# Block 2's state-space stage over 80 units with paired products, the second attention and the gated unit moved behind

## The chip, the cores and the metric

One NeuronCore of a Trainium2 chip runs the whole kernel. The metric is the device time of one execution in microseconds. TensorE multiplies, VectorE (DVE) and ScalarE (ACT) work on tiles in SBUF and PSUM, GpSimd (POOL) on tiles in SBUF, and the SP queue issues the loads of the weights.

## The reference, cut to what matters

Two transformer-like blocks in fp32, on 256 tokens of width 2048. The change is in the second one's mixers:

```python
def second_block(x, ...):
    h = rmsnorm(x, norm1_g)
    proj = h @ w_in                      # 2048 x 12288: uv, s5_in, q, k, v and three gates
    y_a = gmlp_mixer(uv, ...)            # u * (tril(W_s) rmsnorm(v) + b), chunks of 128 tokens
    y_b = s5_mixer(s5_in, ...)           # the state-space stage
    y_c = stick_breaking_attention(q, k, v)      # 8 heads of 128
    br = einsum('blnw,nwd->blnd', stack([y_a, y_b, y_c]), w_branch)
    x = x + sum(gates * br) @ w_out
    h2 = rmsnorm(x, norm2_g)
    x = x + square(relu(h2 @ w_mlp_in)) @ w_mlp_out

def s5_mixer(xin, ...):                  # 64 groups of 16 channels, each with 64 complex states
    bu_re, bu_im = einsum(u, bb_re), einsum(u, bb_im)        # products in, K = 16 per group
    s = associative_scan(s[t] = a * s[t-1] + bu[t])          # complex, over 256 tokens
    y = einsum(s_re, c_re) - einsum(s_im, c_im) + d * xin    # products out
    g = gelu(y)
    return g * sigmoid(g @ w_glu + b_glu)
```

## The kernel before

**Units.** All large products run as "units": a load of 128x1024 fp32 weights by the SP queue into `raw` (a ring of 4), a rounded high half `whi` on ScalarE, the rest `wlo` on VectorE (L946), and 12 matmuls of 128x512 on TensorE (high by high, high by low, low by high). Unit i's high half waits until unit i-4 is multiplied, so ScalarE and VectorE can be at most some three units ahead. There are 1048 units. Block 2's first phase holds 120: 96 for the projections s5, q, k, v, gv, u (two chunks of 8 units each), then 24 for three chunks of gates.

**The order.** Everything else is written by hand as generators that say `yield p`: on each engine, step p of a generator comes behind unit p of that engine (its high half on ScalarE, its low half on VectorE, its matmuls on TensorE), counted from the start of the phase. Within a step the generators run in a fixed order; on VectorE the evictions come first, then the state-space stage, the attention, the gated unit. A step that waits holds up everything behind it on its engine, the next half or unit too.

**The state-space stage** has 32 tiles of 128 states (real and imaginary). Tile j: TensorE puts B·u into bank `PU[j % 2]` (K = 32 rows at a tile position, `s5_in`, step S5Q + 2j, S5Q = 26); VectorE turns it by a table of angles (L1312, L1313 read PSUM and the table; L1315, L1316 combine) and scans over time (L1320, L1321, `ROT`), step S5Q + 2j + 2; GpSimd turns it back into `STATE` (L468 to L471); for each pair of tiles TensorE multiplies by C into `PT[1][:, 0:T]` (`s5_out`, step S5Q + 4m + 9, four column groups of 32); for every four tiles VectorE adds d·x (`skip`, L1328) and releases the bank (`s5_y`). The tables come by SP loads into a ring of 5 in tile G. The stage ends at step 90.

**The second attention** (`attn2`, head h at q0 = HQ2 + 6h, HQ2 = 57): scores into `PT[0]`, Abs, Exp, Ln on ScalarE, L1336 to L1338 on VectorE, the triangle products on TensorE at q0 + 3, Exp on ScalarE, the product with v into `PT[1][:, T:2T]` at q0 + 6, and the high and low half of the result (`y_lo`, L1055) at q0 + 8. `PT[1]` is one bank shared by `s5_out` and this product. So the product waits for the `skip` of all quads multiplied out by then, and `s5_out` for the `y_lo` of the last head.

**The gated unit** (`gmlp`, GQ = 104): squares and root for the norm, the scaling with the gain GMG, four mixing products, the multiplication by u, four transposes. **The gates' evictions** (L1019) read the biases, for n = 0 from `slot(W, 7, 2)`, which is the stage's scratch until its end, and write `GT[k]`, slots of G where the tables lie.

Of the kernel before, what the change touches and what calls it, by code (L numbers as in the profile page):

```python
# [21 lines left out]
P = 128  # L22
# [27 lines left out]
def build(nc, A, out):  # L50
    with ExitStack() as ctx:
# [163 lines left out]
        def yready(b, k):  # L215
# [22 lines left out]
        GMG = slot(W, 6)  # L238
# [20 lines left out]
            slot(W, 8)[:, 0:512], slot(G, 2)[:, 512:1024], slot(Z, 5)[:, 512:1024], slot(Z, 11)[:, 512:1024])]  # L259
# [3 lines left out]
        S5Q, HQ2, GQ = 26, 57, 104  # L263
# [18 lines left out]
        def bias_buf(n, k):  # L282
            if n == 0:
                return slot(W, 7, 2)[:, CH * k:CH * k + CH]
            return slot(W, 12)[:, CH * ((3 * n + k) % 2):CH * ((3 * n + k) % 2) + CH]
# [41 lines left out]
        def _(sp_):  # L327
# [6 lines left out]
            def tables():  # L334

                for j in range(S5_TILES):
                    yield S5Q + 2 * j + 1 if j >= NTAB else 6 + j
                    if j == 0:
                        sp_.wait_ge(S("tables_saved"), 32 * S5_TILES // TG)
                    if j >= NTAB:  # L340
                        sp_.wait_ge(S("s5_state_ready"), j - NTAB + 1)
                    sp_.dma_start(TAB[j % NTAB], A["tables"][j]).then_inc(S(f"table_in{j % NTAB}"), 16)
# [41 lines left out]
        def _(pool):  # L384
# [59 lines left out]
            def block2():  # L444

                pool.wait_ge(S("vA_ready"), 1)
                pool.wait_ge(used, mlp_base(1, NF - 1))
                bsrc = BSRC
                for r, name in enumerate(("s5_b_re_2", "s5_b_im_2")):
                    pool.dma_start(bsrc[:, r], A[name][0].rearrange("(j g) p h -> (g p) j h", g=2)).then_inc(S("small2_in"), 16)  # L450
                csrc = CSRC
                for r, name in enumerate(("s5_c_re_2", "s5_c_im_2")):
                    pool.dma_start(csrc[:, r], A[name][0].rearrange("(i g) h q -> (g h) i q", i=8)).then_inc(S("small2_in"), 16)
                gw = GWSRC
                pool.dma_start(gw, A["gm_w_s_2"][0].rearrange("g t s -> t g s")).then_inc(S("small2_in"), 16)
                pool.wait_ge(evict["dve"], down0[1] + NF * NCH)
                pool.dma_start(A["x1"].rearrange("(t p) n -> p t n", p=P), X).then_inc(S("x_saved"), 16)
                pool.wait_ge(S("small2_in"), 16 * 5)
                nc.gpsimd.affine_select(out=gw, in_=gw, compare_op=ALU.is_ge, fill=0.0, base=0,
                                        pattern=[[0, 8], [-1, P]], channel_multiplier=1).then_inc(S("gm_w_tril"), 1)  # L460
                for j in range(S5_TILES):

                    tab, r, state = TAB[j % NTAB], ROT[j % 2], STATE[j % NS]
                    c, s = (tab[:, i].unsqueeze(1).to_broadcast([P, 2, T]) for i in range(2))
                    pool.wait_ge(S("s5_r_ready"), j + 1)
                    if j >= NS:
                        pool.wait_ge(S("s5_read"), j - NS + 1)
# [79 lines left out]
        def _(act):  # L547
# [72 lines left out]
            def evictions(b):  # L620
# [148 lines left out]
            def s5a():  # L769
# [5 lines left out]
                yield S5Q + 80  # L775
                act.wait_ge(S("s5_y"), 8)
                a(GS, GS, ACT.Gelu_apprx_tanh).then_inc(S("s5_g"), 1)
                for h in range(2):
                    yield S5Q + 82 + h
# [3 lines left out]
            def attn2():  # L783
                for h in range(8):
                    q0 = HQ2 + 6 * h
                    yield q0 + 2
# [6 lines left out]
                    yield q0 + 5  # L793
# [4 lines left out]
                    yield q0 + 8  # L798
                    act.wait_ge(S("sb_mm"), h + 1)
                    a(YH[:, 16 + h, :], PT[1][:, T:2 * T]).then_inc(S("y_hi22"), 1)  # L800

            def gmlp():
                yield GQ - 5
# [6 lines left out]
                yield GQ - 2  # L810
                act.wait_ge(S("gm_ms"), 1)
                a(grs, grs, ACT.Sqrt).then_inc(S("gm_root"), 1)
                for n in range(4):
                    yield GQ + 10 + 2 * n
# [119 lines left out]
        def _(dve):  # L934
# [66 lines left out]
            def evictions(b):  # L1001
# [5 lines left out]
                for ch in plan[b, "a"] + plan[b, "b"]:  # L1007
# [263 lines left out]
            def s5():  # L1271
# [51 lines left out]
                yield S5Q + 72  # L1323
# [6 lines left out]
            def attn2():  # L1330
                for h in range(8):
                    q0 = HQ2 + 6 * h
                    yield q0 + 2
# [5 lines left out]
                    yield q0 + 8  # L1339
                    y_lo(2, 2, 16 + h, 1, PT[1][:, T:2 * T].unsqueeze(1), h + 1)  # L1340

            def gmlp():
                yield GQ - 3
                dve.wait_ge(S("gm_squares"), 2)
                ts(grs, gss, 1.0 / 1024, EPS, ALU.mult, ALU.add).then_inc(S("gm_ms"), 1)
                yield GQ - 2
# [3 lines left out]
                for t in range(NT):  # L1350
                    yield GQ - 1 + t
                    stt(GV[:, t, :], GV[:, t, :], grs[:, t:t + 1], GMG, ALU.mult, ALU.mult).then_inc(S("gm_normed"), 1)

                for n in range(4):
                    yield GQ + 2 * n + 2
# [7 lines left out]
                for n in range(4):  # L1363
                    yield GQ + 10 + 2 * n
                    y_lo(2, 0, 2 * n, 2, PU[n % 2].rearrange("p (k t) -> p k t", t=T), n + 1)

            def s5_g_lo():
                for h in range(2):
                    yield S5Q + 83 + h
# [133 lines left out]
        def _(pe):  # L1503
# [207 lines left out]
            def attn2():  # L1711
                z = PT[0]
                for h in range(8):
                    q0 = HQ2 + 6 * h
# [4 lines left out]
                    else:  # L1719
# [4 lines left out]
                        .then_inc(S("z_mm"), 1)  # L1724
                    yield q0 + 3
# [8 lines left out]
                    yield q0 + 6  # L1734
                    pe.wait_ge(S("sb_w"), h + 1)
                    pe.wait_ge(evict["act"], find[(2, "v", h // 4)].evicted)
                    if h:
                        pe.wait_ge(yready(2, 2), h)
                    if st["s5_out"] >= 4:
                        pe.wait_ge(S("s5_y"), st["s5_out"] // 4)  # L1740
                    y = PT[1][:, T:2 * T]
                    mm(y, VT[:, 0, P * h:P * h + P], A_W[:, 0:T])
                    mm(y[:, P:T], VT[:, 1, P * h:P * h + P], A_W[:, T:3 * P], start=False,
                       skip_group_check=True).then_inc(S("sb_mm"), 1)
                    st["sb"] = h + 1
# [144 lines left out]
```

## Time and profile before

| | us |
|---|---|
| median of 3 runs | 3086.62 (3086.5 to 3095.28) |
| the profiled execution | 3086.01 |
| its span, first to last instruction | 3084.3 |
| TensorE busy | 3040.4 |
| TensorE weight loads busy | 2475.4 |
| VectorE busy | 1998.2 |
| ScalarE busy | 1562.0 |
| GpSimd busy | 498.8 |

The engines work side by side, and their ends of matmuls are modelled, so busy shares alone don't tell where TensorE runs at full rate. A stretch's count of matmuls tells more: the intervals between starts of successive matmuls, and what lies in them.

### The profile page before, as it was taken

What the parts mean: (1) busy time and instruction counts of PE and PEld (TensorE: products, weight loads), DVE (VectorE), ACT (ScalarE), POOL (GpSimd) and SP (SyncE); (2) the same over time, 40 slices, a digit from 0 to 9 for tenths busy, and PEclk for the clock granted to TensorE, in tenths of its full rate; (3) what the DMA queues carried; (4) which work ended last, traced back from release to release, by engine and by line L of the source; (5) the groups of instructions that cost most, each with busy time, mean ns of one, the idle gap of its engine ahead of it and who ended that gap; (6) DMA issues with size and microseconds to landing.
All of it is one profiled execution on the core that took longest, in us unless ns stands there. A gap on an engine that the chain in (4) does not pass through costs nothing.

```text
span 3084.3 us, 37620 instructions
## 1 busy us (share of the span) xinstructions
PE 3040.4 (99%) x13610; PEld 2475.4 (80%) x13610; DVE 1998.2 (65%) x2102; ACT 1562.0 (51%) x2065; POOL 498.8 (16%) x430
## 2 busy tenths in 40 slices
PE   8999999999999999999999999999999999999998
PEld 6777888888888888888877678888888888888886
DVE  5566655556787666666679875555555666666666
ACT  5445544444554555555543456544445555555554
POOL 2000101107882000000048650100100000000000
PEclk9999999999999999999999999999999999999999
DMA  6544666656666666665755445666655666566664
GB/s 197 155 144 145 218 196 199 199 176 218 212 225 217 192 192 194 193 194 187 233 164 165 153 137 181 207 209 202 213 195 184 195 194 191 191 196 191 194 193 150
DMA packets 297642, 585.27 MB, mean 190 GB/s; under 512 B 18520, under 2 KB 18688, under 8 KB 297152
## 3 DMA queue, kind: packets, MB, share of 16 engines
q1 hardware_dynamic: 291328, 562.11, 57.6%
q0 software_dynamic: 6080, 21.70, 2.3%
q8 instruction: 68, 1.11, 0.1%
q14 instruction: 38, 0.31, 0.0%
q10 hardware_dynamic: 128, 0.03, 0.0%
HBM read 571.19 MB, written 12.58 MB: 189 GB/s over the span
## 4 chain that ended last, share of the span: by engine, by line
PE 89%; DVE 6%; issue 2%; ACT 1%; DMA 1%; DVEq 0%; SPq 0%; ACTq 0%
PE banks L1507 88%; DVE wlo L946 3%; PE banks L1510 1%; DMA raw<-in_w_in 1%; ACT whi L556 1%; DVE W L1316 1%; ACT W L556 0%; DVE W L1321 0%; DVE W L1313 0%; DVE W L1312 0%; DMA raw<-in_w_mlp_down 0%; DVE W L1449 0%; ACT XH L556 0%; ACT G L556 0%; DVE XL L997 0%
## 5 line engine op out<-in xcount | busy, mean ns | idle before, releaser
L946 DVE TENSOR_TENSOR wlo<-raw,whi 128x1024 fp32r<-128x1024 f32 x1048 | 1363.3, 1307 | 929.7 <-ACT whi L556 923.1
L556 ACT ACTIVATE whi<-raw 128x1024 fp32r<-128x1024 f32 x1048 | 1101.0, 1059 | 1065.8 <-PE banks L1507 971.7
L1507 PE MATMUL banks<-whi,Y 128*128 128x512 f32 x4800 | 1487.6, 390 | 2.7 <-DVE W L1449 2.5
L1507 PEld LDWEIGHTS banks<-whi,Y 128*128 128x128 f32 x4800 | 900.9, 188 | 191.6 <-issue 2.6
L1507 PE MATMUL banks<-wlo,Y 128*128 128x512 f32 x2400 | 933.8, 389 | 0.0
L1507 PE MATMUL banks<-whi,XH 128*128 128x512 f32 x1792 | 716.4, 400 | 15.2 <-DVE wlo L946 12.4
L1507 PE MATMUL banks<-whi,XL 128*128 128x512 f32 x1792 | 700.5, 391 | 0.0
L1507 PE MATMUL banks<-wlo,XH 128*128 128x512 f32 x1792 | 700.4, 391 | 0.0
L1507 PEld LDWEIGHTS banks<-wlo,Y 128*128 128x128 f32 x2400 | 450.6, 188 | 92.7
L1507 PEld LDWEIGHTS banks<-whi,XH 128*128 128x128 f32 x1792 | 337.8, 188 | 106.7 <-DVE wlo L946 21.1
L1507 PEld LDWEIGHTS banks<-whi,XL 128*128 128x128 f32 x1792 | 337.3, 188 | 72.9
L1507 PEld LDWEIGHTS banks<-wlo,XH 128*128 128x128 f32 x1792 | 337.8, 189 | 65.9
L556 ACT ACTIVATE W<-banks 32x256 f32<-32x256 f32 (+2 forms) x554 | 215.8, 390 | 112.0 <-PE banks L1510 63.1
L1449 DVE SCALAR_TENSOR_TENSOR W<-banks,small,W 128x512 f32<-128x512 f32 x256 | 179.6, 743 | 0.9 <-PE banks L1507 0.9
L535 POOL TENSOR_TENSOR W<-W 128x1024 f32<-128x1024 f32 x20 | 62.8, 3140 | 474.4 <-DVE W L1036 474.4
L450 POOL DMA_DIRECT2D Z<-in_s_b_re x1 | 1.7, 1697 | 517.7 <-PE banks L1507 517.7
L469 POOL TENSOR_TENSOR W<-W,G 128x512 f32<-128x512 f32 x32 | 66.8, 2088 | 0.0
L1507 PE MATMUL banks<-W,Z 32*128 32x256 f32 (+2 forms) x192 | 52.6, 395 | 8.4 <-DVE W L1328 8.4
L1510 PE MATMUL banks<-ident,W 128*128 128x128 f32 x360 | 53.6, 275 | 1.3 <-DMA W<-in_x 0.8
L1510 PEld LDWEIGHTS banks<-ident,W 128*128 128x128 f32 x360 | 44.6, 141 | 12.5 <-DVE W L1449 1.4
L556 ACT ACTIVATE Z<-banks 128x512 f32<-128x512 f32 (+2 forms) x22 | 11.9, 539 | 84.4 <-PE banks L1510 71.6
L1507 PEld LDWEIGHTS banks<-W,Z 32*128 32x128 f32 (+2 forms) x192 | 30.8, 178 | 27.8 <-issue 23.1
(254 smaller groups left out, 1311.7 us busy)
## 6 DMA issues: line engine op xcount, KB each, us to landing
raw<-in_w_in SPq DMA_DIRECT2D x384, 512.0 KB, 3.9
raw<-in_w_mlp_up SPq DMA_DIRECT2D x128, 512.0 KB, 3.7
raw<-in_w_mlp_down SPq DMA_DIRECT2D x128, 512.0 KB, 3.5
raw<-in_w_mlp_in SPq DMA_DIRECT2D x128, 512.0 KB, 3.7
raw<-in_w_mlp_out SPq DMA_DIRECT2D x128, 512.0 KB, 3.5
raw<-in_w_branch SPq DMA_DIRECT2D x80, 512.0 KB, 4.3
raw<-in_w_out SPq DMA_DIRECT2D x64, 512.0 KB, 4.5
tables<-G POOLq DMA_DIRECT2D x8, 1024.0 KB, 8.7
```

The lines of the kernel that those rows point to most:

```text
L450: pool.dma_start(bsrc[:, r], A[name][0].rearrange("(j g) p h -> (g p) j h", g=2)).then_inc(S("small2_in"), 16)
L469: chain(tt(STMP, r, s, ALU.mult))
L535: tt(m, m, TMP[added % 2], ALU.add).then_inc(S("tmp_added"), 1)
L556: return nc.scalar.activation(out_, in_, f, **kw)
L946: tt(wlo[:, i % RING, :], raw[:, i % RING, :], whi[:, i % RING, :].bitcast(F32), ALU.subtract)\
L1316: chain(tt(D1[:, 1], D1[:, 1], D2[:, 0], ALU.subtract))
L1449: ins = stt(x, PA[n % 2][t], r2[:, t:t + 1], x, ALU.mult, ALU.add)
L1507: return nc.tensor.matmul(out_, l, r, start=start, stop=stop, **kw)
L1510: return nc.tensor.transpose(out_, in_, ident[:, :])
```

## The change

The 32 tiles take 80 units instead of 64 (S5D = 5 units a pair). TensorE multiplies both tiles of a pair in at one step, interleaved, into `PU[0]` and `PU[1]`, and a pair out at step 5m + 8 of the stage; VectorE handles the two tiles three and four steps after the product in. The table loads and skips follow. The attention starts at step 70 instead of 57 with 5 units a head instead of 6; a head's product with v and its halves run one step behind the next head's scores. The gated unit starts at 110 instead of 104. The gain and two biases are loaded by GpSimd among tiles 24 to 26 into slots that the attention's first heads have freed, the third bias behind the last tile. The first gate's eviction waits for the last tile three steps later than before.

```diff
-        GMG = slot(W, 6)
+        GMG = slot(W, 11)
...
         STATE = [m.rearrange("p (r t) -> p r t", r=2) for m in (
-            slot(W, 8)[:, 0:512], slot(G, 2)[:, 512:1024], slot(Z, 5)[:, 512:1024], slot(Z, 11)[:, 512:1024])]
+            slot(Z, 5)[:, 512:1024], slot(Z, 11)[:, 512:1024], slot(W, 8)[:, 0:512], slot(G, 2)[:, 512:1024])]
...
-        S5Q, HQ2, GQ = 26, 57, 104
+        S5Q, S5D, HQ2, HD2, GQ = 26, 5, 70, 5, 110
...
             if n == 0:
-                return slot(W, 7, 2)[:, CH * k:CH * k + CH]
+                return slot(W, 9, 2)[:, CH * k:CH * k + CH]
...
                 for j in range(S5_TILES):
-                    yield S5Q + 2 * j + 1 if j >= NTAB else 6 + j
+                    yield S5Q + S5D * (j // 2) - (0 if j % 2 else 3) if j >= NTAB else 6 + j
...
                     pool.wait_ge(S("s5_state_ready"), j + 1)
-
-                pool.wait_ge(S("s5_read"), 32)
-                pool.dma_start(GMG, A["gm_norm_g_2"][0].partition_broadcast(P)).then_inc(S("gm_gain_in"), 16)
-                for k in range(3):
-                    load_bias(0, k)
+                    if j in (24, 25, 26):
+                        pool.wait_ge(S("z_mm"), 4)
+                        if j == 24:
+                            pool.dma_start(GMG, A["gm_norm_g_2"][0].partition_broadcast(P)).then_inc(S("gm_gain_in"), 16)
+                        else:
+                            load_bias(0, j - 25)
+
+                pool.wait_ge(S("z_mm"), 8)
+                load_bias(0, 2)
```

On ScalarE:

```diff
-                        yield end_of(b, ch) + 4
+                        yield end_of(b, ch) + (4 if ch.tag[1:] != (0, 0) else 7)
...
-                yield S5Q + 80
+                yield S5Q + 87
                 act.wait_ge(S("s5_y"), 8)
...
             def attn2():
                 for h in range(8):
-                    q0 = HQ2 + 6 * h
-                    yield q0 + 2
+                    q0 = HQ2 + HD2 * h
+                    yield q0 + 3
                     act.wait_ge(S("z_mm"), h + 1)
...
-                    yield q0 + 5
+                    if h:
+                        yield q0 + 4
+                        y_hi(h - 1)
+                    yield q0 + 6
                     act.wait_ge(S("tri_mm"), h + 1)
```

On VectorE:

```diff
                         n, k = ch.tag[1:]
+                        dve.wait_ge(S(f"bias_in{k}"), 16 * (n + 1))
+                        if n == 0 and k == 0:
+                            yield end_of(b, ch) + 6
+                            dve.wait_ge(S("s5_state_ready"), 32)
                         dve.wait_ge(used, ch.u0 + ch.nu)
-                        dve.wait_ge(S(f"bias_in{k}"), 16 * (n + 1))
-                        if n == 0:
-                            dve.wait_ge(S("s5_state_ready"), 32)
...
                 for j in range(32):
-                    if j >= 7 and j % 4 == 3:
-                        yield S5Q + 2 * j + 1
+                    if j % 4 == 2 and j > 2:
+                        yield S5Q + S5D * (j // 2) + 1
                         skip(j // 4 - 1)
-                    yield S5Q + 2 * j + 2
+                    yield S5Q + S5D * (j // 2) + 3 + j % 2
...
-                yield S5Q + 72
+                yield S5Q + 86
                 skip(7)
```

On TensorE:

```diff
             def s5_in():
-                for j in range(32):
-                    yield S5Q + 2 * j
-                    i, c = j // 4, 32 * (j % 4)
-                    if j == 0:
+                for m in range(16):
+                    yield S5Q + S5D * m
+                    i, c0 = m // 2, 64 * (m % 2)
+                    if m == 0:
                         pe.wait_ge(S("s5_mT_copied"), 8)
                         pe.wait_ge(S("stage_copied"), sbase[2] + 4)
-                    if j >= 2:
-                        pe.wait_ge(S("s5_bu_read"), j - 1)
+                    else:
+                        pe.wait_ge(S("s5_bu_read"), 2 * m)
                     for r in range(2):
-                        ins = mm(PU[j % 2][:, T * r:T * r + T], BT[r][c:c + 32, i, :], XI[c:c + 32, i, :],
-                                 tile_position=(c, 0))
-                    ins.then_inc(S("bu_mm"), 1)
+                        for e in range(2):
+                            c = c0 + 32 * e
+                            ins = mm(PU[e][:, T * r:T * r + T], BT[r][c:c + 32, i, :], XI[c:c + 32, i, :],
+                                     tile_position=(c, 0))
+                    ins.then_inc(S("bu_mm"), 2)
 
             def s5_out():
                 for m in range(16):
-                    yield S5Q + 4 * m + 9
+                    yield S5Q + S5D * m + 8
...
                     mm(z[:, T:3 * P], KT2[:, h, P:T], QT2[:, h, P:T], start=False, skip_group_check=True)\
                         .then_inc(S("z_mm"), 1)
+                    if h:
+                        yield q0 + 1
+                        product(h - 1)
                     yield q0 + 3
...
-                    yield q0 + 6
-                    pe.wait_ge(S("sb_w"), h + 1)
...
+                yield q0 + 6
+                product(7)
+
+            def product(h):
+
+                pe.wait_ge(S("sb_w"), h + 1)
+                pe.wait_ge(evict["act"], find[(2, "v", h // 4)].evicted)
+                if h:
+                    pe.wait_ge(yready(2, 2), h)
+                if st["s5_out"] >= 4:
+                    pe.wait_ge(S("s5_y"), st["s5_out"] // 4)
```

VectorE's attention step moves to q0 + 3 and its `y_lo` of head h-1 to q0 + 4. The gated unit's steps keep their distances from GQ but for one unit: on VectorE the scalings come at GQ and GQ + 1 (before GQ - 1 and GQ) and the multiplications by u at GQ + 2n + 3 (before + 2), on ScalarE the squares at GQ - 3 (before GQ - 5), while TensorE's stay at GQ + 2n and GQ + 8 + 2n.

## Rows read from the trace of the kernel before

**Rows 1.** The head of the page: busy us (share of the span) xinstructions of each engine.

```profile
PE 3040.4 (99%) x13610; PEld 2475.4 (80%) x13610; DVE 1998.2 (65%) x2102; ACT 1562.0 (51%) x2065; POOL 498.8 (16%) x430
```

**Rows 2.** Stretches: us; busy PE, PEld, DVE, ACT, POOL; PEclk, DMA share, GB/s.

```profile
1565.61:1930.41 364.80, 353.59 (x1609) 267.41 (x1608) 297.20 (x357) 173.15 (x203) 197.45 (x132) 0.98 0.51 159
1975.86:2008.50 32.64, 32.64 (x145) 27.03 (x144) 17.77 (x16) 12.73 (x12) 6.53 (x2) 1.00 0.78 248
1597.96:1691.31 93.35, 91.77 (x409) 65.64 (x409) 92.05 (x99) 32.85 (x39) 76.03 (x49) 1.00 0.54 169
1700.63:1723.30 22.67, 18.49 (x75) 13.57 (x73) 16.86 (x22) 8.58 (x12) 15.47 (x12) 0.85 0.47 151
1806.20:1829.03 22.83, 18.61 (x76) 13.60 (x74) 17.02 (x22) 8.64 (x12) 15.56 (x12) 0.85 0.42 127
```

**Rows 3.** Timeline of TensorE: start us, us, engine line op out<-in xcount.

```profile
1604.61 0.39 PE L1507 MATMUL banks<-whi,XL 128*128 128x512 f32 x1
1604.92 1.13 PE L1507 MATMUL banks<-W,Z 32*128 32x256 f32 x4
1605.98 0.50 PE L1507 MATMUL banks<-whi,XH 128*128 128x512 f32 x1
1606.32 0.39 PE L1507 MATMUL banks<-wlo,XH 128*128 128x512 f32 x1
...
1845.37 0.81 PE L1507 MATMUL banks<-W,Z 128*128 128x256 f32 x4
...
1846.60 0.48 PE L1507 MATMUL banks<-whi,XH 128*128 128x512 f32 x1
...
1852.26 1.06 PE L1507 MATMUL banks<-Z 128*32 128x256 f32 x8
1853.25 0.50 PE L1507 MATMUL banks<-whi,XH 128*128 128x512 f32 x1
...
1856.15 0.59 PE L1507 MATMUL banks<-W,NLOW 128*128 128x256 f32 x2
...
1857.38 0.48 PE L1507 MATMUL banks<-whi,XH 128*128 128x512 f32 x1
```

**Rows 4.** The same timeline at the first hole; in brackets the idle time and what ended it.

```profile
1715.56 1.62 PE L1507 MATMUL banks<-W,Z 128*128 128x256 f32 x4 [4.18 <-DVE W L1328]
...
1718.11 0.77 PE L1507 MATMUL banks<-whi,XH 128*128 128x512 f32 x1
...
1720.39 0.54 PE L1507 MATMUL banks<-whi,XL 128*128 128x512 f32 x1
```

**Rows 5.** Timeline of VectorE, one tile and its two low halves.

```profile
1604.43 3.44 DVE L946 TENSOR_TENSOR wlo<-raw,whi 128x1024 fp32r<-128x1024 f32 x2
1607.80 0.68 DVE L1312 TENSOR_TENSOR W<-banks,G 128x512 f32<-128x512 f32 x1
...
1610.45 1.11 DVE L1320 TENSOR_TENSOR_SCAN W<-small,W 128x256 f32<-128x256 f32 x1
1611.49 0.66 DVE L1321 TENSOR_TENSOR_SCAN W<-small,W 128x256 f32<-128x256 f32 x1
1612.18 1.23 DVE L946 TENSOR_TENSOR wlo<-raw,whi 128x1024 fp32r<-128x1024 f32 x1
```

**Rows 6.** Views of single lines, 1565.6 to 1930.4: duration ns min/median/max, first and last start us.

```profile
L1316 DVE TENSOR_TENSOR W<-W x32: 412/956/968, 1571.7 to 1830.9; 128x256 f32<-128x256 f32 x32
L469 POOL TENSOR_TENSOR W<-W,G x32: 1259/2273/2292, 1575.8 to 1835.0; 128x512 f32<-128x512 f32 x32
L471 POOL TENSOR_TENSOR Z<-Z,W x16: 730/914/1717, 1594.6 to 1838.0; 128x256 f32<-128x256 f32 x16
```

**Rows 7.** Timelines of ScalarE and VectorE, the first head's chain from scores to Ln.

```profile
1687.31 0.49 ACT L556 ACTIVATE W<-banks 128x384 f32<-128x384 f32 x1 [5.63 <-PE banks L1507]
...
1690.95 0.52 ACT L556 ACTIVATE W<-W 128x384 f32<-128x384 f32 x1
...
1691.51 0.56 DVE L1336 SCALAR_TENSOR_TENSOR W<-banks,W 128x384 f32<-128x384 f32 x1 [0.26 <-ACT W L556]
```

More of the change, by code:

```diff
@@ L778, in s5a @@
                 for h in range(2):
-                    yield S5Q + 82 + h
+                    yield S5Q + 88 + h
                     act.wait_ge(S("s5_g"), 1)
@@ L797, in attn2, with y_hi @@
                     a(A_W, PT[0][:, 0:384], ACT.Exp).then_inc(S("sb_w"), 1)
-                    yield q0 + 8
-                    act.wait_ge(S("sb_mm"), h + 1)
-                    a(YH[:, 16 + h, :], PT[1][:, T:2 * T]).then_inc(S("y_hi22"), 1)
+                yield q0 + 9
+                y_hi(7)
+            def y_hi(h):
+                act.wait_ge(S("sb_mm"), h + 1)
+                a(YH[:, 16 + h, :], PT[1][:, T:2 * T]).then_inc(S("y_hi22"), 1)
             def gmlp():
-                yield GQ - 5
+                yield GQ - 3
                 act.wait_ge(S("s5_bu_read"), 32)
@@ L809, in gmlp @@
                     act.wait_ge(S("gm_squares"), t + 1)
-                yield GQ - 2
+                yield GQ - 1
                 act.wait_ge(S("gm_ms"), 1)
@@ L813, in gmlp @@
                 for n in range(4):
-                    yield GQ + 10 + 2 * n
+                    yield GQ + 11 + 2 * n
                     act.wait_ge(S("gm_T"), n + 1)
@@ L1331, in attn2 @@
                 for h in range(8):
-                    q0 = HQ2 + 6 * h
-                    yield q0 + 2
+                    q0 = HQ2 + HD2 * h
+                    yield q0 + 3
                     dve.wait_ge(S("ln_ready"), h + 1)
@@ L1338, in attn2 @@
                     tt(A_E[:, 2 * P:3 * P], A_E[:, 2 * P:3 * P], S01[:, :], ALU.mult).then_inc(S("sp_ready"), 1)
-                    yield q0 + 8
-                    y_lo(2, 2, 16 + h, 1, PT[1][:, T:2 * T].unsqueeze(1), h + 1)
+                    if h:
+                        yield q0 + 4
+                        y_lo(2, 2, 15 + h, 1, PT[1][:, T:2 * T].unsqueeze(1), h)
+                yield q0 + 9
+                y_lo(2, 2, 23, 1, PT[1][:, T:2 * T].unsqueeze(1), 8)
             def gmlp():
-                yield GQ - 3
+                yield GQ - 2
                 dve.wait_ge(S("gm_squares"), 2)
                 ts(grs, gss, 1.0 / 1024, EPS, ALU.mult, ALU.add).then_inc(S("gm_ms"), 1)
-                yield GQ - 2
+                yield GQ - 1
                 dve.wait_ge(S("gm_root"), 1)
@@ L1350, in gmlp @@
                 for t in range(NT):
-                    yield GQ - 1 + t
+                    yield GQ + t
                     stt(GV[:, t, :], GV[:, t, :], grs[:, t:t + 1], GMG, ALU.mult, ALU.mult).then_inc(S("gm_normed"), 1)
                 for n in range(4):
-                    yield GQ + 2 * n + 2
+                    yield GQ + 2 * n + 3
                     t, g0 = n // 2, 4 * (n % 2)
@@ L1363, in gmlp @@
                 for n in range(4):
-                    yield GQ + 10 + 2 * n
+                    yield GQ + 11 + 2 * n
                     y_lo(2, 0, 2 * n, 2, PU[n % 2].rearrange("p (k t) -> p k t", t=T), n + 1)
@@ L1368, in s5_g_lo @@
                 for h in range(2):
-                    yield S5Q + 83 + h
+                    yield S5Q + 89 + h
                     dve.wait_ge(S("s5_g_hi"), h + 1)
@@ L1713, in attn2 @@
                 for h in range(8):
-                    q0 = HQ2 + 6 * h
+                    q0 = HQ2 + HD2 * h
                     yield q0
@@ L1733, in attn2 @@
                     mm(z[:, T:3 * P], ident[:, :], SM[:, :], **kw).then_inc(S("tri_mm"), 1)
-                    yield q0 + 6
-                    pe.wait_ge(S("sb_w"), h + 1)
[L1736 to L1745, printed above, removed]
+                yield q0 + 6
[3 more added lines that the diff above has]
+                pe.wait_ge(evict["act"], find[(2, "v", h // 4)].evicted)
+                if h:
+                    pe.wait_ge(yready(2, 2), h)
+                if st["s5_out"] >= 4:
+                    pe.wait_ge(S("s5_y"), st["s5_out"] // 4)
+                y = PT[1][:, T:2 * T]
+                mm(y, VT[:, 0, P * h:P * h + P], A_W[:, 0:T])
+                mm(y[:, P:T], VT[:, 1, P * h:P * h + P], A_W[:, T:3 * P], start=False,
+                   skip_group_check=True).then_inc(S("sb_mm"), 1)
+                st["sb"] = h + 1
             def gmlp():
```

## The prediction

> **What bounds the kernel now.** I read the head of the page first, then tables of stretches, then TensorE, VectorE, GpSimd and ScalarE in the one stage that the change touches. TensorE is busy 99% of the span [rows 1], so an edit pays only where TensorE has less to do or where it waits. A "unit" is twelve 128x512 products of a split weight. In a quiet stretch 32.64 us hold 12 units [rows 2], so a unit costs 2.72 us. The stage and what follows it, units 26 to 119 of block 2's first phase, take 364.8 us for 94 units [rows 2]; 94 x 2.72 is 255.7, so 109 us are small products between units and waiting. Nowhere else does the change touch anything.
>
> Three readings say what the 109 us are. (1) One state-space tile's product in: the last unit matmul starts at 1604.61, the next unit at 1605.98, where two matmuls of a quiet unit lie 2.72 / 12 = 0.23 apart, and its second follows 0.34 later [rows 3]: 1.37 - 0.23 + 0.11, with the third's share 1.27 us, 32 times. A pair of tiles out takes 0.99 (1852.26 to 1853.25) and 0.27 at its edges, 1.26 us, 16 times; an attention head takes 1.23 (1845.37 to 1846.60) and an edge of 0.13 for its product and the next scores, and as much for its triangle products (1856.15 to 1857.38): 1.36 each [rows 3]. (2) Two holes. At 1715.56 TensorE has waited 4.18 us for the skip addition of VectorE (L1328) [rows 4]. `skip` reads the same bank (PT[1]) into which the attention product writes, and VectorE has a whole tile ahead of it in its order. After the wait the granted clock falls to the lower level (0.85 in the mean of that stretch, and again in the stretch at 1806 [rows 2]): product and scores then take 2.55 us to the next unit (1715.56 to 1718.11) instead of 1.23, and the unit's first five matmuls 2.28 (to 1720.39) instead of 1.2 [rows 3, 4]. 4.2 + 1.3 + 1.1 is 6.6 us a hole, 13.2 for both. (3) VectorE is busy 92.05 of 93.35 us from 1597.96 on, GpSimd 76.03 [rows 2], so the stage's first part runs at VectorE's pace, though hardly slower than TensorE's: TensorE's busy time of 353.59 leaves 11.2 us idle, of which the holes are 8.4 and 2.8 are waits for low halves, since TensorE's own extra work nearly fills the time.
>
> **The change part by part.** Two tiles now share five units instead of four, and TensorE puts both products in side by side (row groups 0 and 32, or 64 and 96, into two banks) instead of one at a time.
>
> *TensorE.* Products in: 16 pairs instead of 32 singles. No row shows two row groups side by side. The nearest is the pair out, where two column groups start 8 instructions within 0.99 us, as long as 4 single ones of the product in (1.06) [rows 3]. I take 1.26 a pair: 32 x 1.27 - 16 x 1.26 = 20.5 us saved; from the other side, nothing saved if the pair runs serially. The Trainium skill ("TensorE: Matmul & The Clock Gate", Part 3) says that matmuls in different row groups run concurrently, with starts about 4 ns apart; no row here shows it for rows. The split of product and scores into two places costs one more edge of 0.1 to 0.2 us a head, but the product follows the product in directly; I count it at nothing, up to +1.5. The units, the pairs out, the triangles and the gated unit's products are as many as before. Three of the gated unit's transposes move behind unit 120, +1.4 us there, which the same sum takes off here.
>
> *The holes.* The product of head h-1 now stands at q0+1, and the skip that it needs one step later in VectorE's order, with no tile ahead of it. VectorE runs one to three units ahead, so the low half of the next unit and the skip (0.5 us) end before TensorE gets there. Both holes go, 13.2 us. The last product (step 111) waits for skip 7 (step 112), the scores of head h+1 for an Exp one step later in ScalarE's order, the gated unit's first product (110) for a scaling at 111: each of these waits has half a unit or more to spare, where VectorE isn't late.
>
> So were TensorE alone the bound, the stretch would take 364.8 - 20.5 - 13.2 - 2.8 = 328.3 us, 36.5 less.
>
> *VectorE, and what the others do to it.* In the full stretch a tile with two low halves takes 7.75 us (1604.43 to 1612.18) [rows 5]. A low half alone takes 1.15, but the two took 3.37 to the next start; L1316 takes 0.956 at the median and 0.412 at the least, L1320 1.11 where its twin L1321 takes 0.66 [rows 5, 6]. GpSimd stretches likewise: L469 1.26 at the least and 2.27 at the median, L471 0.73 and 0.91 [rows 6]. Where both read SBUF, one stands still. VectorE thus loses 1.07 + 0.54 + 0.45, about 2.1 us a tile, to GpSimd's about 4.0 (2 x 1.26 + 2 x 0.73); the rest passes beneath its reads from PSUM (L1312, L1313) and in part overlaps. Own work is 7.75 - 2.1 - 2.3 = 3.35 a tile. Five units then want 2 x 3.35 + 5 x 1.15 + 0.25 (half a skip) = 12.7, and blocking: the least 0, as before 4.2, all of it 8.0. The first tile of a pair has the second's PSUM reads beside it, as now; the second tile's GpSimd work meets four low halves in a row, so I take 2.1 + 2.9: 17.7 us. TensorE wants 13.6 + 1.26 + 1.26 = 16.1, 16.6 with the transposes that lie here. The Trainium skill ("SBUF — State Buffer", on the shared port pair) calls it an exclusive lock for a whole instruction, against a VectorE operation with two SBUF inputs; the doubled durations agree. By it nothing but PSUM reads would be free: that is the lock rival below, priced there from rows.
>
> Nine such periods before the attention (units 26 to 70): 1.1 us over TensorE's each, less 3 us since VectorE starts three units ahead: +7.
>
> Seven periods with a head each (71 to 105): TensorE 16.1 + 2.7 = 18.8. ScalarE's chain from scores to the Ln takes 1687.31 to 1691.47, with two table loads in it, and VectorE's first attention step then starts at 1691.51 [rows 7]. VectorE goes on with about 1.5 us of attention work and 0.4 of `y_lo`, ahead of or behind the pair's first tile: 17.7 + 1.9 = 19.6, +0.8 a period, +5.6. `s5_out` waits for that `y_lo`, behind a 4.5 us tile; TensorE has three units and a triangle until then, so it is covered.
>
> The gated unit, the gate's eviction put three steps back (GT[0] lies on the tables), and the squares on ScalarE: fewer VectorE steps per unit than in the periods before. +1.
>
> *DMAs.* GpSimd now issues three loads among tiles 24 to 26 behind a wait for scores 4, which are some two periods old by then; about 0.6 us each on an engine with 6 us a period to spare; behind them wait only the state work and then the pairs out, 8 steps off. The SP queue's table loads wait for a tile five back, which GpSimd ends about when they are reached; raw loads behind them stand a period ahead. Nothing.
>
> Sum: 328.3 + 7 + 5.6 + 1 = 341.9 in the stretch, + 1.4 behind it: 21.5 less than 364.8. Against the profiled execution's own time (3086.0, of it 3084.3 span): 3064.5; the median of the runs shown lies 0.6 above it. I say 3064.
>
> **The rivals.**
> - *TensorE is the bound everywhere.* VectorE has a fifth unit's time to catch up and GpSimd's work falls apart from it: 3086 - 36.5 + 1.4, 3051. For it: holes were the larger part of today's waiting. Against: VectorE is full at 1597 to 1691. Chance 0.18.
> - *Pairs in run serially.* 16 x 1.14 more for TensorE, of which 0.8 to 1.1 a period lies beneath VectorE's excess: +4 to +8, 3070. Or one or two holes stay, at unit 110 or 111 or a head: 6.6 each, 3071 to 3077. Chance together 0.18.
> - *Lock.* GpSimd's state work (L468 to L471) blocks VectorE for all its 4.0 us a tile but 1.2 beneath the PSUM reads once a period: 12.7 + 6.8 = 19.5 before the attention, 21.4 with it: +2.9 x 9 - 3, +2.6 x 7, +1: 3051 + 42 = 3093, no change. With no cover at all, 8.0: 20.7 and 22.6, +34 + 27 + 1: 3113, slower. It decides against the change from a blocking of about 6.3 us a period on, where TensorE waits 2.2 us a pair over 16 pairs. Chance 0.12 for 3078 to 3095, 0.04 beyond.
> - *A hole at every head*, at its product behind the skip or its scores behind the Exp: 7 x 6.6 on 3064 = 3110. It needs VectorE less than 2 us ahead at each head. Chance 0.04.
>
> **How the numbers follow.** The forecast has 0.44 (3056 to 3070). About 0.3% (9 us) is what a measurement of this kernel can tell from no change. Faster by more (under 3077): 0.44 + 0.18 + 0.18 = 0.80; within: 0.12; slower: 0.08. The range takes in the TensorE bound with a few us for less blocking, 3046, and reaches into the lock rival, to 3084.
>
> **What would show it.** 128 products of 32 rows that start in pairs, and 1.0 us from the first of eight to the next unit; else the pairing is wrong. No wait of TensorE on L1328 and a granted clock of 1.00 all along, else the holes are. VectorE near 100% busy in units 30 to 70, 17.7 us per pair, and TensorE about 1 us a pair idle; 19.6 with a head. If L946 stays near 1.2 us and pairs take 16.6, the first rival is right; if it takes 2.3 for most units, the lock. Waits of TensorE at units 110 or 111 that don't exist today would be the change's own.

## The result, and the profile after

The changed kernel takes 3059.5 us in the median (3057.0 to 3060.9) against 3087.6 before (3086.5 to 3095.3): the ratio is 0.9901, with a 95% interval of 0.989 to 0.9913. The forecast was 3064 in a range from 3046 to 3084. The profiled execution took 3058.6 us, 3056.9 of it span, 27.4 less span than before.

Lines of the changed kernel lie lower in the file: L957 makes the low halves (L946 before), L1522 the matmuls (L1507), L1324 to L1333 the state-space tile (L1312 to L1321).

The head of its page, which answers to [rows 1]:

```profile
PE 3018.5 (99%) x13610; PEld 2463.8 (81%) x13610; DVE 2014.7 (66%) x2102; ACT 1562.6 (51%) x2064; POOL 503.6 (16%) x430
```

As many matmuls as before, with 22 us less of TensorE's busy time. The table of stretches, as in [rows 2], first for units 26 to 119, then for its three parts (units 26 to 70, 71 to 105, 106 to 119) and the 18 units behind:

```profile
1568.70:1901.55 332.85, 328.43 (x1598) 252.99 (x1596) 311.54 (x355) 172.42 (x199) 203.83 (x132) 1.00 0.57 176
1568.70:1724.01 155.31, 150.89 (x713) 112.67 (x711) 149.98 (x157) 57.65 (x66) 110.06 (x69) 1.00 0.57 176
1724.01:1855.30 131.29, 131.29 (x655) 101.97 (x655) 128.14 (x151) 83.69 (x101) 89.58 (x61) 1.00 0.56 172
1855.30:1901.55 46.25, 46.25 (x234) 38.36 (x232) 33.42 (x49) 31.08 (x33) 4.20 (x4) 1.00 0.59 184
...
1901.55:1953.90 52.35, 52.35 (x245) 43.29 (x244) 31.69 (x35) 27.06 (x37) 5.07 (x4) 1.00 0.54 178
```

The same parts of the kernel before:

```profile
1565.61:1747.43 181.82, 175.92 (x778) 128.41 (x776) 167.41 (x191) 69.18 (x83) 134.76 (x88) 0.98 0.50 159
1747.43:1887.58 140.15, 134.84 (x626) 103.14 (x625) 103.06 (x132) 81.33 (x96) 62.69 (x45) 0.98 0.50 155
1887.58:1930.41 42.83, 42.83 (x211) 35.87 (x210) 26.74 (x36) 22.64 (x25) 0.00 (x0) 1.00 0.56 172
...
1930.41:1981.30 50.89, 50.89 (x233) 42.11 (x232) 30.72 (x33) 25.61 (x34) 5.07 (x4) 1.00 0.59 193
```

The stretch falls from 364.8 to 332.85 us, by 32.0; the 18 units behind it take 1.5 more. That is 30.5. The span shows 27.4, because the stretch begins 3.1 us later: that was lost in block 1, where nothing was changed (last section).

The product of a pair in, in the timeline of TensorE of the changed kernel, against the one tile in [rows 3]:

```profile
1640.41 0.39 PE L1522 MATMUL banks<-whi,XL 128*128 128x512 f32 x1
1640.73 1.13 PE L1522 MATMUL banks<-W,Z 32*128 32x256 f32 x8
1641.80 0.50 PE L1522 MATMUL banks<-whi,XH 128*128 128x512 f32 x1
```

Eight instructions in the time of four: 1.07 us to the next unit, where a single tile's four take 1.06. In the trace the eight start two by two, the second of each two 7 ns behind the first.

What holds TensorE up in the stretch, from the table of waits of the changed kernel (us in total, times, longest):

```profile
PE banks L1522 <- DVE wlo L957: 4.3, 7, 1.4
```

No wait on the skip is left; these seven are low halves, all before unit 71, about one a pair. VectorE in turn waits for nothing between its low halves for units 36 and 66 (no gap of 0.15 us or more). The same stretch of the changed kernel between TensorE's starts of these units:

```profile
1603.28:1706.76 103.48, 100.93 (x476) 74.68 (x476) 102.25 (x106) 38.72 (x44) 77.67 (x49) 1.00 0.59 183
```

These are six pairs at 17.25 us, and TensorE takes as long from unit 36 to 66 as VectorE takes from the end of one low half to that of the other. So before the attention VectorE sets the pace.

### The profile page after: what moved, and what is told of

It is laid out like the page before. It is cut to its first block, busy times and chain, and to the rows that moved or that the text cites. A ratio compares the mean times of both kernels' runs of the same rounds, so it can differ in the third digit from the quotient of the medians.

```text
span 3056.9 us, 37623 instructions
## 1 busy us (share of the span) xinstructions
PE 3018.5 (99%) x13610; PEld 2463.8 (81%) x13610; DVE 2014.7 (66%) x2102; ACT 1562.6 (51%) x2064; POOL 503.6 (16%) x430
## 4 chain that ended last, share of the span: by engine, by line
PE 90%; DVE 6%; issue 2%; ACT 1%; DMA 1%; DVEq 0%; SPq 0%; ACTq 0%
PE banks L1522 89%; DVE wlo L957 2%; PE banks L1525 1%; DMA raw<-in_w_in 1%; ACT whi L560 1%; DVE W L1328 0%; DVE W L1333 0%; DVE W L1324 0%; DVE W L1325 0%; ACT W L560 0%; DVE W L1464 0%; ACT XH L560 0%; ACT G L560 0%; DVE XL L1008 0%; DVE W L1131 0%
## 5 line engine op out<-in xcount | busy, mean ns | idle before, releaser
L957 DVE TENSOR_TENSOR wlo<-raw,whi 128x1024 fp32r<-128x1024 f32 x1048 | 1378.9, 1322 | 921.7 <-ACT whi L560 915.6
L1522 PE MATMUL banks<-whi,Y 128*128 128x512 f32 x4800 | 1489.9, 390 | 4.3 <-DVE W L1464 4.1
L1522 PEld LDWEIGHTS banks<-whi,Y 128*128 128x128 f32 x4800 | 902.0, 188 | 193.4 <-issue 4.6
L1522 PE MATMUL banks<-wlo,Y 128*128 128x512 f32 x2400 | 934.5, 389 | 0.0
L1522 PE MATMUL banks<-whi,XH 128*128 128x512 f32 x1792 | 714.6, 399 | 16.7 <-DVE wlo L957 14.0
L1522 PE MATMUL banks<-whi,XL 128*128 128x512 f32 x1792 | 699.5, 390 | 0.0
L1522 PE MATMUL banks<-wlo,XH 128*128 128x512 f32 x1792 | 699.4, 390 | 0.0
L1522 PEld LDWEIGHTS banks<-wlo,Y 128*128 128x128 f32 x2400 | 451.1, 188 | 92.7
L1522 PEld LDWEIGHTS banks<-whi,XH 128*128 128x128 f32 x1792 | 337.0, 188 | 105.3 <-issue 18.3
L1522 PEld LDWEIGHTS banks<-whi,XL 128*128 128x128 f32 x1792 | 336.8, 188 | 72.7
L1522 PEld LDWEIGHTS banks<-wlo,XH 128*128 128x128 f32 x1792 | 337.3, 188 | 65.8
L1464 DVE SCALAR_TENSOR_TENSOR W<-banks,small,W 128x512 f32<-128x512 f32 x256 | 179.6, 743 | 0.9 <-PE banks L1522 0.9
L469 POOL TENSOR_TENSOR W<-W,G 128x512 f32<-128x512 f32 x32 | 62.8, 1963 | 0.0
L468 POOL TENSOR_TENSOR Z<-W,G 128x512 f32<-128x512 f32 x16 | 33.3, 2079 | 118.3 <-DVE W L1333 84.7
```

The costliest lines, as they stand in the source:

```text
L957: tt(wlo[:, i % RING, :], raw[:, i % RING, :], whi[:, i % RING, :].bitcast(F32), ALU.subtract)\
L1464: ins = stt(x, PA[n % 2][t], r2[:, t:t + 1], x, ALU.mult, ALU.add)
L1522: return nc.tensor.matmul(out_, l, r, start=start, stop=stop, **kw)
```

## The experiments

The tables below give, of each profile, the three parts (26 to 70, 71 to 105, 106 to 119) and the whole way from unit 26 to unit 138, by the starts of the units in the timeline of TensorE. Block 1 lies outside, so its 3 us don't disturb the comparison.

| kernel | 26-70 | 71-105 | 106-119 | 26-138 | median us |
|---|---|---|---|---|---|
| before | 181.8 | 140.2 | 42.8 | 415.7 | 3086 to 3090 |
| the change | 155.3 | 131.3 | 46.3 | 385.2 | 3059.5 |
| e1_unpaired | 160.2 | 140.1 | 46.3 | 399.0 | 3071.5 |
| e2_heads_earlier | 180.4 | 136.0 | 42.7 | 410.0 | 3084.7 |
| e3_pairs_only | 187.2 | 139.7 | 42.8 | 420.6 | 3093.4 |
| e4_skip_behind_tile | 156.3 | 153.2 | 46.3 | 408.1 | 3081.6 |
| e5_gpsimd_one_of_four | 148.4 | 131.2 | 46.3 | 378.2 | 3048.7 |
| e6_tiles_apart | 149.6 | 130.8 | 46.2 | 379.0 | 3053.7 |
| e7_pairs_even | 179.5 | 138.2 | 42.8 | 411.5 | 3085.1 |
| e8_change_again | 155.3 | 131.3 | 46.3 | 385.1 | 3059.8 |
| e9_apart_again | 149.6 | 130.8 | 46.2 | 378.9 | 3055.2 |

**e1: the change without pairs.**

```diff
-                for m in range(16):
-                    yield S5Q + S5D * m
+                for j in range(32):
+                    yield S5Q + S5D * (j // 2) + j % 2
...
-                        for e in range(2):
-                            c = c0 + 32 * e
-                            ins = mm(PU[e][:, T * r:T * r + T], BT[r][c:c + 32, i, :], XI[c:c + 32, i, :],
+                        ins = mm(PU[j % 2][:, T * r:T * r + T], BT[r][c:c + 32, i, :], XI[c:c + 32, i, :],
```

> The changed kernel, but each tile's product in by itself, the second of a pair one unit later. My theory: 16 x 1.14 = 18 us more for TensorE, of which some 6 us lie beneath what VectorE costs anyway before the attention (units 26 to 70), so 12 us more than the changed kernel, about 3071 us; units 71 to 105 grow from 131 to 139 us. Rival A, VectorE is the bound everywhere: at most 3 us more. Rival B, TensorE is the bound everywhere: 18 us more, 3078 us.

Measured: 3071.5 us, ratio to the kernel before 0.9938 (0.9922 to 0.9955). Units 71 to 105 grow by 8.8 us, seven pairs at 1.26; units 26 to 70 by 4.9, where nine pairs at 1.14 would be 10.3. My theory holds in both parts. In the table of stretches e1's TensorE is busy all the time:

```profile
1569.48:1729.68 160.20, 160.14 (x713) 118.26 (x712) 151.12 (x159) 57.51 (x65) 111.59 (x70) 1.00 0.57 174
1729.68:1869.82 140.14, 140.14 (x657) 105.84 (x656) 125.46 (x150) 83.74 (x101) 86.10 (x60) 1.00 0.53 161
```

So of the 30.5 us between units 26 and 138, 13.8 hang on the pairs with the new spacing in place, and 16.7 come from everything else in the change: the spacing, the places of the attention and the gated unit, and the two holes.

**e2: the kernel before, without its holes.** `S5Q, HQ2, GQ = 26, 57, 104` becomes `26, 56, 104`.

> The kernel before, with the second attention one unit earlier (HQ2 = 56), so that no head's product stands right behind the end of a group of four tiles out. My theory: both holes go, with their lower clock, 13.2 us: about 3074 us, and no wait of TensorE on the skip over 1 us. Rival: a hole lets VectorE get ahead (its low halves were ready 8.6 us early behind each), and without it VectorE's pace costs TensorE the same time in small waits: 5 us or less gained, 3082 us or more.

Measured: 3084.7 us, ratio 0.9985 (0.9975 to 0.9994). The rival's number was right: 5.7 us from unit 26 to 138 and not 13.2. The two waits of 4.2 us on L1328 are gone, and in their place TensorE's timeline has

```profile
1697.06 0.75 PE L1507 MATMUL banks<-whi,XH 128*128 128x512 f32 x1 [2.93 <-DVE wlo L946]
...
1719.92 0.41 PE L1507 MATMUL banks<-Z 128*32 128x256 f32 x2 [0.95 <-DVE Y L1055]
...
1770.43 0.38 PE L1507 MATMUL banks<-W,Z 128*32 128x256 f32 x1 [1.04 <-DVE Y L1055]
...
1821.52 0.63 PE L1507 MATMUL banks<-Z 128*32 128x256 f32 x4 [1.55 <-DVE Y L1055]
```

and a spell of 3.4 us at the lower clock behind the first of them. But the rival's reason, that without the holes VectorE comes late, isn't in this trace. The wait of 2.93 us stands at unit 59, four units ahead of where the first hole was: step 58, where the first head's work on VectorE now stands, already has a tile, and VectorE does 4.4 us of tile and 2.7 of attention in a row ahead of the low half:

```profile
1692.39 0.66 DVE L1321 TENSOR_TENSOR_SCAN W<-small,W 128x256 f32<-128x256 f32 x1
1693.08 0.56 DVE L1336 SCALAR_TENSOR_TENSOR W<-banks,W 128x384 f32<-128x384 f32 x1
...
1695.79 2.88 DVE L946 TENSOR_TENSOR wlo<-raw,whi 128x1024 fp32r<-128x1024 f32 x2
```

Behind it, in units 60 to 70, the low halves are 3 to 6 us early. The other three, 3.5 us, are pairs out that wait for a head's `y_lo`, which none does in the kernel before. All four come with the heads' new place. Priced like the holes they are 2.9 + 3.5 + 1.7 (the spell), 8.2 us, and the two holes with their spells 6.8 each, 13.6: 5.4 us less, 5.7 measured. So the edit took the holes out at their full price and brought others in.

**e3: the kernel before, with pairs only.**

```diff
-                for j in range(32):
-                    yield S5Q + 2 * j
+                for m in range(16):
+                    yield S5Q + 4 * m
...
-                    yield S5Q + 2 * j + 2
+                    yield S5Q + 2 * j + 2 - j % 2
```

> The kernel before, with only the products in paired (a pair every four units, the odd tile one step earlier on VectorE). TensorE has 20 us less to do. My theory: VectorE, full already at four units a pair, gives little of it back: 15.5 us a pair stay 15.5 before the attention; 3 to 8 us gained, 3079 to 3084 us, and the holes stay. Rival: TensorE is the bound and the whole 20 us are gained, 3066 us; the fifth unit would then be needless.

Measured: 3093.4 us, ratio 1.0013 (1.0004 to 1.0023). Neither: TensorE has 20 us less to do, and the kernel gets slower, 4.9 us from unit 26 to 138. Both forecasts fail. The stretch's own row:

```profile
1569.07:1756.27 187.20, 167.95 (x781) 124.51 (x779) 173.06 (x191) 69.20 (x83) 124.60 (x87) 0.96 0.50 151
```

VectorE is idle 14 us and TensorE 19. But VectorE was idle 14 us in the kernel before too; what grew by as much as the stretch (5.4 us) is its busy time, from 167.4 to 173.1 us (5.7), for the same instructions. TensorE waits 17.9 us for low halves, once a pair or nearly. Here is what VectorE did in its timeline, and then the end of the wait in TensorE's:

```profile
1595.06 0.68 DVE L1312 TENSOR_TENSOR W<-banks,G 128x512 f32<-128x512 f32 x1
1595.66 0.68 DVE L1313 TENSOR_TENSOR W<-banks,G 128x512 f32<-128x512 f32 x1
1596.37 1.45 DVE L1315 TENSOR_TENSOR W<-W 128x256 f32<-128x256 f32 x1
1597.74 0.96 DVE L1316 TENSOR_TENSOR W<-W 128x256 f32<-128x256 f32 x1
1598.73 1.10 DVE L1320 TENSOR_TENSOR_SCAN W<-small,W 128x256 f32<-128x256 f32 x1
1599.75 0.66 DVE L1321 TENSOR_TENSOR_SCAN W<-small,W 128x256 f32<-128x256 f32 x1
1600.45 5.66 DVE L946 TENSOR_TENSOR wlo<-raw,whi 128x1024 fp32r<-128x1024 f32 x3
```

```profile
1601.73 0.65 PE L1507 MATMUL banks<-whi,XH 128*128 128x512 f32 x1 [2.92 <-DVE wlo L946]
```

The second tile of the pair takes 5.4 us (1595.06 to 1600.45), with GpSimd's work on the first inside it, and the low half for which TensorE waits stands behind both. From this I formed theory B: two tiles close together on VectorE make TensorE wait, although VectorE's total work would fit. The row shows only half of that. VectorE's waits for products in do grow, from 3.2 to 9.3 us, since TensorE comes late to them; but in the sum of its idle time they take the place of others.

**e4: the change with the skip behind the tile.** This brings holes back.

```diff
-                    if j % 4 == 2 and j > 2:
-                        yield S5Q + S5D * (j // 2) + 1
-                        skip(j // 4 - 1)
...
                     dve.wait_ge(S("s5_r_ready"), j + 1)
+                    if j % 4 == 2 and j > 2:
+                        skip(j // 4 - 1)
```

> The changed kernel, but each skip behind the next pair's first tile on VectorE instead of two steps ahead of it. My theory: three holes, at the products of heads 1, 3 and 5 (steps 81, 91, 101), each a wait of 4 to 5 us and a spell at the lower clock, 6.6 us each: 20 us more than the changed kernel, 3079 us. Rival: the spell at the lower clock doesn't come or the wait is made up by VectorE's getting ahead: 3 x 4.5 us or less, 3073 us or below.

Measured: 3081.6 us, ratio 0.9977 (0.9967 to 0.9987). Three holes, at steps 81, 91 and 101, and 21.9 us more in units 71 to 105: 7.3 each. From its table of waits and of stretches:

```profile
PE banks L1521 <- DVE W L1339: 17.3, 3, 6.6
```

```profile
1722.84:1876.06 153.22, 135.88 (x654) 105.33 (x655) 122.94 (x152) 83.78 (x101) 87.95 (x63) 0.93 0.51 153
```

The waits are 6.65, 5.33 and 5.33 us, longer than the 4.2 of [rows 4], and the granted clock is 0.93 in the mean, three spells of 6.8 us at the lower level. So the place of one operation of 0.5 us on VectorE, two steps later, takes back 22 of the change's 30 us. Nothing of a hole is given back here, where TensorE and not VectorE sets the pace: the waits are 17.3 us, and 9.0 us of TensorE's work at half the clock behind them cost 4.5 more, 21.8 of the 21.9.

**e5: GpSimd with one operation of four.** The product with the cosine (L468) is kept; the product with the sine and the two sums (L469 to L471) are left out.

> The changed kernel, with one of GpSimd's four state operations a tile left (the product with the cosine; the sine products and the sums are left out, so the states are not the reference's). My theory: what TensorE still waits for before the attention is VectorE, slowed by GpSimd in SBUF: L957 falls from 1.66 us in the mean to under 1.35, units 26 to 70 from 155.3 to 149 to 151 us, units 71 to 105 stay at 131 us; 5 us less in all. Rival: the waits come from the two tiles standing close together on VectorE, whatever GpSimd does: units 26 to 70 keep 154 us or more.

Measured: 3048.7 us, ratio 0.9872 (0.9856 to 0.9888). Units 26 to 70 take 148.4 us, with TensorE busy to the last hundredth, and units 71 to 105 stay at 131.2:

```profile
1564.93:1713.33 148.40, 148.40 (x714) 113.06 (x712) 123.75 (x159) 57.55 (x65) 39.03 (x18) 1.00 0.60 188
```

TensorE's 148.4 in the first part is thus what it needs by itself, and 6.9 us of the change's 155.3 are VectorE's with GpSimd's blocking. The low halves fell less than I had said, from 1.66 to 1.45 us in the mean over units 26 to 119; VectorE's whole busy time fell by 26 us in this part. 3.8 of the 10.8 us in the time are block 1's, where the stretch begins earlier (1564.93 against 1568.70). The rival, that the waits stay whatever GpSimd does, is out.

**e6 and e9: tiles apart.**

```diff
-                    yield S5Q + S5D * (j // 2) + 3 + j % 2
+                    yield S5Q + S5D * (j // 2) + 3 + 2 * (j % 2)
...
-                    yield S5Q + S5D * m + 8
+                    yield S5Q + S5D * m + 9
```

> The changed kernel, with the odd tile of a pair one unit later on VectorE (3 and 5 units behind the product in instead of 3 and 4) and the pair out one unit later. Theory V, VectorE's total work with GpSimd's blocking is the bound before the attention (it is 97% busy there): units 26 to 70 stay at 154 to 156 us. Theory B, tile, low half, tile, low half in a row make TensorE wait once a pair: 150 to 152 us, 4 us less in all.

> The changed kernel itself, beside the next one on the same chip: 3057 to 3061 us.

> The changed kernel with the tiles of a pair two units apart on VectorE (as in e6_tiles_apart), beside the changed kernel. Theory B: 4 to 6 us less than the changed kernel, since units 26 to 70 lose their waits for low halves. Rival: the 5 us between the earlier runs were the spread of the wait in block 1 (near 935 us); then the two agree within 2 us.

Measured: 3053.7 us, ratio 0.989 (0.9874 to 0.9907); then beside the change on one chip 3055.2 against 3059.8 us, ratios to the kernel before of 0.9886 (0.9871 to 0.9902) and 0.9906 (0.9893 to 0.992). The two intervals overlap, but every run of e9 (3050.7 to 3056.5) lies below every run of the change beside it (3056.8 to 3063.7), and the traces don't leave the difference open: units 26 to 70 take 149.6 us in both profiles of e6 and e9, and 155.3 in both of the change. That is theory B's number, or a little less. The row of e6:

```profile
1568.14:1717.77 149.63, 148.92 (x713) 113.09 (x712) 144.37 (x154) 57.53 (x65) 110.77 (x68) 1.00 0.62 185
```

The row also says that theory B's reason is wrong for the changed kernel. VectorE is busy 144.4 of 149.6 us, 96 to 97% as before the edit, and again it waits for nothing between units 36 and 66. It has the same instructions as in the change, but they take 5.6 us less. The costliest groups whose time moved, first in the change, then in e6, for units 26 to 70:

```profile
L957 DVE TENSOR_TENSOR wlo<-raw,whi 128x1024 fp32r<-128x1024 f32 x46 | 76.1, 1693 | 7.7 <-ACT whi L560 7.0
L1327 DVE TENSOR_TENSOR W<-W 128x256 f32<-128x256 f32 x18 | 16.9, 940 | 0.6
```

```profile
L957 DVE TENSOR_TENSOR wlo<-raw,whi 128x1024 fp32r<-128x1024 f32 x45 | 79.2, 1800 | 7.6 <-ACT whi L560 7.0
L1327 DVE TENSOR_TENSOR W<-W 128x256 f32<-128x256 f32 x18 | 8.8, 489 | 0.6
```

In the change the second tile of a pair meets GpSimd's work on the first: L1327 takes 1.46 us there (at 1632.40) and 0.42 in the first tile. With the odd tile one unit later it takes 0.43 in both from unit 36 on, and the low halves take back half of what that saves. From the end of low half 36 to that of low half 66 VectorE takes 103.5 us in the change and 100.5 in e6, 17.25 and 16.76 a pair; TensorE in e6 takes 16.62. So VectorE's pace was the limit in the change, and the edit shortened it; even in e6 VectorE is slightly slower than TensorE and lives on its lead until unit 65. Theory V failed only in taking GpSimd's blocking for fixed: it depends on what meets what.

This version is the fastest that computes the reference, by 6.2 us against the changed kernel from unit 26 to 138.

**e7: e3 with the odd tile back in its place**, `yield S5Q + 2 * j + 2`.

> The kernel before with paired products in, the odd tile on VectorE left where it was (every second unit), so that the next pair in waits for its reads. Theory B, what cost the pairs at four units was the two tiles close together (VectorE was busy only 173 of 187 us there and TensorE idle 19 us): units 26 to 70 fall from 187 to 180 us or below and the time is 3083 us or less, below the kernel before. Theory V, VectorE's total work at four units a pair: 182 us or more, 3086 us or more.

Measured: 3085.1 us, ratio 0.9985 (0.9975 to 0.9994); units 26 to 70 take 179.5 us against 187.2 of e3. For this part the number is theory B's (180 or below), for the time it isn't: 3083 or less was expected. Of the 7.7 us about half is again VectorE's busy time (173.1 to 169.2 us) and half its idle time (14.1 to 10.3), so here, where TensorE and VectorE wait for each other in turn, the order counts by itself too. Even so only 2.3 us of the ten or so that the pairs save TensorE in this part reach the time: TensorE is busy 164.8 of the 179.5 us and VectorE 169.2, at most pairs TensorE waits 0.9 and 0.5 us for a low half, and the two holes are still there (4.18 and 4.36 us). At four units a pair VectorE can hardly follow in either order tried; the fifth unit is what lets the pairs pay.

## Why the prediction was right, and where its steps were off

- **The bound from TensorE's side: right.** The periods said 9 x 16.6, 149.4 us, for units 26 to 70 and 7 x 18.8, 131.6 us, for 71 to 105, if nothing waits; with most of GpSimd's load taken away (e5) the trace shows 148.4 and 131.2, and for the whole stretch 325.9 where the sum said 328.3. The pair in costs 1.26 to 1.28 us with its edges, as taken from the pair out, eight instructions in 1.07 us. The Trainium skill ("TensorE: Matmul & The Clock Gate", Part 3) says that products in different row groups run side by side, with starts some 4 ns apart; the trace agrees, with 7 ns.
- **The gain by pairs: right in size, and not by itself.** In the changed schedule the pairs are worth 13.8 us (e1), of the 20.5 of TensorE's work; in the old schedule they cost 4.9 (e3), or are worth 4.2 with the tiles evenly spaced (e7). The text took both parts of the change at once, TensorE's whole saving less VectorE's excess, and for that sum it was enough; the gain belongs to the pairs and the fifth unit together.
- **The holes: right.** Both are gone, and the clock is 1.00 over the stretch. The step "4.2 + 1.3 + 1.1 is 6.6 us a hole" priced TensorE's loss well: by the trace it is the wait of 4.2 and some 2.6 for the 5.1 to 5.3 us of work at the lower clock, 6.8. The clock fell earlier than the text has it, within the wait: the granted clock is 1.00 up to 1713.86 and 0.50 from there to 1720.69, while the product starts at 1715.56. As an edit to the kernel before, the heads' move by one unit was worth 5.7 and not 13.2 (e2), by the 8.2 us of waits that the new place brought. Put back into the changed kernel, a hole costs its whole price, 7.3 (e4). The sum was safe from such exchanges, since it took all of TensorE's waits out at once, which leaves TensorE's needs, and put VectorE's excess in anew.
- **VectorE before the attention: right in its mechanism, the size in part by luck.** Forecast 149.4 + 7, measured 155.3, of which 6.9 are VectorE's (e5). The period of VectorE's throughput was put at 17.7 us and is 17.25, with VectorE never waiting (units 36 to 66). Over e5's 16.55 for the same units that is 0.7 us a pair and not 1.1. On the other side, the 3 us that VectorE's lead should have saved didn't show: the first five units alone take 1.5 us more than in e5, with a wait of 1.35 at unit 31. The text's 9.9 less 3 and the trace's 5.4 (the other eight pairs) plus 1.5 come to the same 7. What the text lacked is that the blocking isn't a property of the work: the same instructions in another order take 5.6 us less (e6).
- **VectorE beside the attention: the term that was mis-sized.** "19.6, +0.8 a period, +5.6" was 0: 131.3 us for seven periods is 18.76 each, TensorE's 18.8. VectorE is busy 128.1 there, 18.3 a period. The text had added the attention's 1.9 us to a period with the same blocking as before; but L1327, 0.94 us in the mean before the attention, takes 0.50 beside it. With the gated unit's +1, which was 0 too (46.3 us in the change and in e5), and TensorE's own 2.4 too many, this makes up the 9 us between the 341.9 of the sum and the 332.9 measured.
- **Outside the stretch.** The 1.4 us behind it were 1.5. Unforeseen, and no part of the change, are the 3.1 us in block 1, which by chance brought the time nearer to the forecast than the stretch was: the forecast is 9.0 us too high there and 5.9 in the span.
- **GpSimd's lock: smaller than the rival, as taken.** The Trainium skill ("SBUF — State Buffer", Who interferes with whom) calls the port pair that VectorE and GpSimd share an exclusive lock, held for a whole instruction. Single instructions of the changed kernel agree, L957 between 1.21 and 2.32 us. As a price for the stage it came to 6.9 us (e5), and by order alone it fell to 1.2 (e6). The rival that charged nearly all of GpSimd's work to VectorE's throughput gave 3093 us, 33 above what was measured.

## What to carry to other kernels

When two engines are both nearly full, sum each one's needs in the new order; don't only subtract the old order's waits, since the new places bring their own (13.2 us on paper, 5.7 in the run, 8.2 us of new waits between them). An engine that is full is not full for good when another engine stretches its instructions: VectorE had no wait left at 17.25 us a pair, and a different order of the same work gave 16.76. So look at the durations of equal instructions for the long ones and what they meet, and try to move them, before taking the engine's pace as given. A wait that depends on a later step of another engine's order is harmless as long as nothing long stands ahead of that step; one tile put ahead of a 0.5 us operation cost 22 us.

## What the runs showed of the hardware that I had not expected

In block 1's second half, while GpSimd makes the tables, TensorE waits near 935 us for VectorE's additions (L1449, L1464 in the changed kernel), in the kernel before 1.33 us and in the changed one 3.30:

```profile
933.54 0.49 PE L1507 MATMUL banks<-whi,Y 128*128 128x512 f32 x1 [1.33 <-DVE W L1449]
```

```profile
935.25 0.50 PE L1522 MATMUL banks<-whi,Y 128*128 128x512 f32 x1 [3.30 <-DVE W L1464]
```

The instructions are the same there. Of eleven profiles eight had 2.9 to 3.35 us and three (before, e4, e5) 1.3. Behind the long wait seven of the eight had a spell at the lower clock, of 3.4 us in six and 6.8 in e9; e6 had none there, and the three short ones had none. e6 and e8 had a spell of 3.4 us at 293 us, too. With the long wait VectorE's instructions ahead of it were longer (the low half at 930.39 took 3.40 us in the changed kernel, the one at 929.18 2.92 in the kernel before), beside GpSimd's; the stretch then begins 1.6 to 7.3 us later than in the three others, at 1568.1 to 1572.2 us against 1564.9 to 1566.6. What decides it in an execution stays open. It is about as large as the scatter of the medians here, so a part of a kernel is better compared by its own starts than by the whole time.

Not every long wait lowered the clock: in e3, waits of 2.47 and 2.92 us were followed by 3.4 us at the lower level, a wait of 3.27 at 1787.83 by none.
